# Seven-product down chunks in eight (and five) turns in a row, with two of their weight differences on GpSimd

## The chip, the cores and the metric

The kernel runs on one core of a Trainium2 chip. The metric is the device time of one execution in microseconds (us). Three executions of the kernel before took 1177.59, 1177.66 and 1177.66 us, median 1177.66.

## The reference, cut to what matters

The model is a two-layer decoder trunk on 256 tokens of 1024 features. Each layer has a half SwiGLU block, a mixer, cross-attention and a second half SwiGLU block, so there are four SwiGLU blocks (called f = 0 to 3 here). The change touches only these:

```python
def swiglu(h, w_gate, w_up, w_down):
    return (jax.nn.silu(h @ w_gate) * (h @ w_up)) @ w_down
x = x + 0.5 * swiglu(rmsnorm(x, w), w_gate, w_up, w_down)   # h: (256, 1024), D_FF = 2816
```

All values are float32. The kernel keeps that precision by splitting every operand of a matmul in a rounded high part and a low rest (hi = round(a), lo = a - hi) and by adding three products, hi*hi, hi*lo and lo*hi.

## The kernel before, in words

A SwiGLU block is cut along D_FF into 11 pieces of 256 (FJ = 11). Each piece j has three weight chunks of 1 MB (128 partitions x 2048 float32): gate g(j), up u(j) and down d(j). Chunks come from memory in the order g(j+1), u(j+1), d(j) into a ring of three slots (`raw`), issued by SyncE's queue (L690). ScalarE writes the high part of a chunk (L889), VectorE the low part (L1616, L1586, L1648, L1667), and only then does the slot take the next load: SyncE waits for `lo_done`.

A turn handles one piece. TensorE's turn j + 1 runs g(j+1) (32 matmuls: 16 with 512 columns, L2334, and 16 with 256, L2341), u(j+1) (32 more) and then the down product of d(j) (L2313 to L2315). ScalarE and VectorE run turn j beside it: gate sum (L1514) and scale (L1519), silu, split of g(j+1), up sum (L1525), product (L1533), split of u(j+1), split of the product into `gu_hi` and `gu_lo`, split of d(j). Gate sum and up sum read PSUM and one SBUF tile; the other VectorE operations here read two SBUF tiles.

The down product multiplies the 256x256 piece of the hidden values (2x2 blocks of 128) by the 256x1024 chunk (2x2 blocks of 128x512). Done plainly it takes eight block products, each of three matmuls (24). In a mixed turn (`turn_mixed`, `turn_mixed_next`, `mixed_down`) it takes seven (21 matmuls), by the scheme of Strassen and Winograd. That needs differences of the weight blocks (four `w_sum`s, L1549, 128x512) and of the hidden blocks (four `gu_sum`s, L1555, 128x128), the high and low parts of three weight sums (L900 on ScalarE, L1607 or L1641 on VectorE, 128x1536) and of three hidden sums (L913, L1538, L1636). All eight differences are VectorE's. One of them overwrites a block of the raw chunk in place.

Four of the seven products go to PSUM banks 0 to 3, which the next g and u need. ScalarE copies them out (banks 0 and 1 at L908, 2 and 3 at L918), VectorE does so after the last mixed turn (`mixed_out`, L1566). In blocks 1 to 3 the copies are summed into `xn` by accumulating DMAs of GpSimd's queue (L2269). GpSimd does nothing else in a SwiGLU block; it computes the norms' factors (L2198, L2200) between them.

Which turns are mixed is fixed by `Mixed.FIRST` and `Mixed.COUNT`: in blocks 1 to 3 turns 1, 2, 3, 5, 6, 7 and 8 (turn 4 is plain), in block 0 turns 4, 6 and 8. That makes 24 mixed down products out of 44.

Of the kernel before, what the change touches and what calls it, by code (L numbers as in the profile page):

```python
# [33 lines left out]
FJ = DFF // CW  # L34
# [130 lines left out]
def build(nc, d, out):  # L165
# [3 lines left out]
    with ctx:  # L169
# [274 lines left out]
        class Mixed:  # L444
            FIRST, COUNT = (2, 0, 0, 0), (3, 7, 7, 7)
            w_sums = part(3072, [3, 512])
            gu_sums = part(4608, [3, P])
# [4 lines left out]
            kept = [copied, kept_later, kept_later, kept_later]  # L452
# [53 lines left out]
        w_summed = [quarters_lo] + [es["dtT_done"]] * 3  # L506
        w_sums_hi = [quarters_hi] + [es["ln_done"]] * 3
        gu_summed = [up_half_in] + [es["o_ssq"]] * 3
        mixed_mm = [halves_hi] + [es["dec_mm"]] * 3
        mixed_read = [quarter_in[0]] + [es["kz_done"]] * 3  # L510
        kept_added_in = [sem(f"kept_added_in{half}") for half in range(2)]

        def kept_added_at(f, i):

            return ((f - 1) * (Mixed.COUNT[f] - 2) + i - 1) * 16

        def mixed_end(f):

            return Mixed.FIRST[f] + Mixed.COUNT[f]

        def counted(f, i, each, first, extra=0):

            return (i - Mixed.FIRST[f]) * each + (1 + (f - 1) * (Mixed.COUNT[f] * each + extra) if f else first)

        def w_sums_at(f, i):
            return counted(f, i, 4, 4)

        def w_sums_hi_at(f, i):
            return counted(f, i, 1, 3)

        def gu_sums_at(f, i):
            return counted(f, i, 4, 16)

        def mixed_mm_at(f, i):
            return counted(f, i, 1, 3)

        def mixed_read_at(f, i):
            return counted(f, i, 2, 16, 8)
# [115 lines left out]
        def _(sp):  # L654
# [13 lines left out]
            def ffn(layer, which, first=False):  # L668
                base = at["ffn", layer, which]
# [15 lines left out]
                def turn(j):  # L685
                    for c, (w, width, row) in enumerate(((gate, CW, j + 1), (up, CW, j + 1), (down, D, j))):
                        n = base + 2 + c
                        if not (first and isinstance(j, int) and j == 0 and c == 0):
                            sp.wait_ge(lo_done, j * 3 + (n - RING + 1))
# [8 lines left out]
                if first:  # L698
# [7 lines left out]
                    for j in range(2, 6):  # L706
                        turn(j)
                        for dst, src in tables[3 * (j - 2):3 * (j - 1)]:
                            sp.dma_start(dst, src).then_inc(small_in, 16)
                    for j, (a, b) in ((6, (0, 4)), (7, (4, 7))):  # L710
                        turn(j)
# [3 lines left out]
                with sp.Fori(8 if first else 0, FJ - 1) as j:  # L715
                    turn(j)
# [21 lines left out]
        def _(act):  # L738
# [115 lines left out]
            def ffn(layer, which):  # L854
# [29 lines left out]
                def turn(j, between=lambda c: None, mixed=None, out=None, added=False):  # L884
# [13 lines left out]
                    def sums_hi():  # L898
                        act.wait_ge(w_summed[f], w_sums_at(f, mixed) + 4)
                        nc.scalar.activation(Mixed.w_hi, Mixed.w_sums, ACT.Copy).then_inc(w_sums_hi[f], 1)  # L900

                    if mixed is not None and out is None and f == 0:
                        sums_hi()
                    if out is not None:
                        act.wait_ge(mixed_mm[f], mixed_mm_at(f, out) + 1)
                        if added and (f > 1 or not isinstance(out, int) or out > 1):
                            act.wait_ge(kept_added_in[0], kept_added_at(f, out))
                        nc.scalar.activation((Mixed.copied if added else Mixed.kept[f])[0], ps[:, 0:2, :],  # L908
                                             ACT.Copy).then_inc(mixed_read[f], 1)
                    act.wait_ge(chunks_used, j * 3 + (base + 2))  # L910
                    if mixed is not None:
                        act.wait_ge(gu_summed[f], gu_sums_at(f, mixed) + 4)
                        nc.scalar.activation(Mixed.gu_hi, Mixed.gu_sums, ACT.Copy)  # L913
                    hidden(j + (f * FJ + 1), gu_hi)
                    if out is not None:
                        if added and (f > 1 or not isinstance(out, int) or out > 1):
                            act.wait_ge(kept_added_in[1], kept_added_at(f, out))
                        nc.scalar.activation((Mixed.copied if added else Mixed.kept[f])[1], ps[:, 2:4, :],  # L918
                                             ACT.Copy).then_inc(mixed_read[f], 1)
                    if mixed is not None and (f or out is not None):  # L920
                        sums_hi()
                    split(base + 4 + RING)
# [27 lines left out]
                if f == 0:  # L950
# [5 lines left out]
                         mixed=2)  # L956
                    turn(5, out=2)
                    turn(6, mixed=3)
                    turn(7)
                    turn(8, mixed=4)  # L960
                    turn(9, small_tables)
                else:
                    turn(1, mixed=0)
                    turn(2, mixed=1, out=0)
                    turn(3, mixed=2, out=1, added=True)
                    turn(4, out=2, added=True)
                    turn(5, mixed=3)
                    with act.Fori(4, 7) as i:
                        turn(i + 2, mixed=i, out=i - 1, added=True)
                    turn(9)  # L970
# [382 lines left out]
        def _(dve):  # L1353
# [154 lines left out]
            def ffn(layer, which):  # L1508
# [33 lines left out]
                slot = raw[:, (base + 4) % RING, :].rearrange("p (a c) -> p a c", c=512)  # L1542
                gu_blocks = gu.rearrange("p (a c) -> p a c", c=P)

                def w_sum(i, c, dst, a, b):

                    if c:
                        dve.wait_ge(w_summed[f], w_sums_at(f, i) + c)
                    V.tensor_tensor(dst, a, b, ALU.subtract).then_inc(w_summed[f], 1)  # L1549
# [1616 lines left out]
```

## Time and profile before

| | |
|---|---|
| median of three runs | 1177.66 us |
| span of the profiled execution (first to last instruction) | 1175.6 us |
| TensorE busy | 1169.0 us (99%) |
| VectorE busy | 957.0 us (81%) |
| ScalarE busy | 727.7 us (62%) |
| GpSimd busy | 131.0 us (11%) |

The profile gives for the execution its span and no time of its own beside it; the median is 2.1 us above the span, which lies before the first and after the last instruction. A busy share is an average over the whole kernel. To know what a SwiGLU turn is bound by one reads the turn itself: how long TensorE's turn is, how full VectorE is in it, and how long before its use each part is ready. The page's timeline of the span in 40 slices shows TensorE's granted clock at 9 (90% or more) in every slice.

### The profile page before, as it was taken

The page shows a single profiled execution, that of the slowest core. Times are in us where ns is not written, and L with a number is a line of the kernel's source. Part 1 is how long each engine was busy: PE and PEld are TensorE (multiplying, and loading weights), DVE is VectorE, ACT ScalarE, POOL GpSimd, SP SyncE. Part 2 cuts the span into 40 slices and gives each one's busy share as a digit, 9 for nine tenths or more (in the row PEclk, how much of TensorE's full clock was granted, in tenths as well). Part 3 has the DMA queues.
Part 4 walks back from the last instruction along what each step waited for, and adds up shares of the span by engine and source line. Part 5 has one row for each costly group of instructions (what it writes and reads, how often), then busy time and mean ns, then how long its engine had stood idle before and what let it go on. Part 6 is the DMA issues. An engine that isn't in the chain of part 4 may idle for free.

```text
span 1175.6 us, 17562 instructions
## 1 busy us (share of the span) xinstructions
PE 1169.0 (99%) x6769; PEld 1022.7 (87%) x6769; DVE 957.0 (81%) x1144; ACT 727.7 (62%) x967; POOL 131.0 (11%) x127
## 2 busy tenths in 40 slices
PE   9999999999999999999999999999999999999998
PEld 8888889889989888888888888889887898888886
DVE  6687898875657589889988979997886676797998
ACT  7566555854457566667565757564576566675773
POOL 1010001420142010100010001010012121100000
PEclk9999999999999999999999999999999999999999
DMA  9966755454445455979765779947623434678891
GB/s 322 332 207 199 200 194 179 145 179 144 144 143 180 144 181 173 270 218 268 226 202 166 229 217 263 269 145 213 209 89 135 135 118 156 208 225 251 245 258 69
DMA packets 168337, 230.71 MB, mean 196 GB/s; under 512 B 15312, under 2 KB 139600, under 8 KB 168144
## 3 DMA queue, kind: packets, MB, share of 16 engines
q1 hardware_dynamic: 163664, 213.30, 55.9%
q0 software_dynamic: 4464, 16.25, 7.3%
q8 instruction: 44, 0.72, 0.3%
q10 hardware_dynamic: 144, 0.26, 0.1%
q14 instruction: 21, 0.17, 0.0%
HBM read 213.02 MB, written 1.05 MB: 182 GB/s over the span
## 4 chain that ended last, share of the span: by engine, by line
PE 99%; POOL 0%; DVE 0%; issue 0%; POOLq 0%; DVEq 0%
PE ps L2334 30%; PE ps L2341 16%; PE ps L2313 15%; PE ps L2314 15%; PE ps L2315 15%; PE ps L2417 1%; PE ps L2611 1%; PE ps L3075 1%; PE ps L2931 1%; PE ps L3098 0%; PE ps L2619 0%; PE ps L3111 0%; PE ps L3036 0%; PE ps L3033 0%; PE ps L2485 0%; PE ps L2683 0%
## 5 line engine op out<-in xcount | busy, mean ns | idle before, releaser
L2334 PE MATMUL ps<-hT,w_parts 128*128 128x512 f32 x1568 | 374.9, 391 | 0.0
L2334 PEld LDWEIGHTS ps<-hT,w_parts 128*128 128x128 f32 x1568 | 290.0, 188 | 58.2 <-ACT w_parts L807 0.4
L1368 DVE TENSOR_TENSOR w_parts<-raw,w_parts 128x2048 fp32r<-128x2048 f32 x85 | 196.1, 2316 | 57.9 <-ACT w_parts L754 57.9
L2341 PEld LDWEIGHTS ps<-hT,w_parts 128*128 128x128 f32 x1568 | 201.4, 191 | 8.0 <-DVE w_parts L1444 0.2
L754 ACT ACTIVATE w_parts<-raw 128x2048 fp32r<-128x2048 f32 x85 | 162.3, 1920 | 72.8 <-PE ps L2315 69.8
L889 ACT ACTIVATE w_parts<-raw 128x2048 fp32r<-128x2048 f32 x108 | 206.0, 1907 | 0.6 <-DMA raw<-in_ffn_w_gate 0.6
L2341 PE MATMUL ps<-hT,w_parts 128*128 128x256 f32 x1568 | 204.1, 283 | 0.0
L1616 DVE TENSOR_TENSOR w_parts<-raw,w_parts 128x2048 fp32r<-128x2048 f32 x63 | 143.9, 2284 | 1.2 <-ACT w_parts L889 1.2
L2313 PE MATMUL ps<-w_parts,arena_r 128*128 128x512 f32 (+1 forms) x234 | 91.2, 390 | 0.0
L2314 PE MATMUL ps<-w_parts,arena_r 128*128 128x512 f32 (+1 forms) x234 | 91.1, 389 | 0.0
L2313 PE MATMUL ps<-w_parts,hT 128*128 128x512 f32 (+1 forms) x240 | 91.0, 379 | 0.0
L2315 PE MATMUL ps<-w_parts,arena_r 128*128 128x512 f32 (+1 forms) x234 | 90.6, 387 | 0.0
L2315 PE MATMUL ps<-w_parts,hT 128*128 128x512 f32 (+1 forms) x240 | 90.1, 375 | 0.0
L2314 PE MATMUL ps<-w_parts,hT 128*128 128x512 f32 (+1 forms) x240 | 90.0, 375 | 0.0
L2269 POOL DMA_DIRECT2D xn<-arena x30 | 26.2, 872 | 386.5 <-ACT arena L908 348.9
L869 ACT ACTIVATE arena<-arena 128x512 f32<-128x512 f32 x44 | 27.7, 630 | 55.9 <-DVE arena L1519 55.8
L1667 DVE TENSOR_TENSOR w_parts<-raw,w_parts 128x2048 fp32r<-128x2048 f32 x21 | 48.1, 2289 | 13.9 <-ACT w_parts L889 13.9
L876 ACT ACTIVATE arena<-ps 128x512 f32<-128x512 f32 x44 | 26.3, 597 | 50.1 <-PE ps L2341 49.1
L2198 POOL TENSOR_SCALAR msq<-msum 128x1 f32<-128x1 f32 x18 | 13.4, 742 | 370.9 <-ACT xn L765 288.1
L862 ACT ACTIVATE arena<-ps 128x512 f32<-128x512 f32 x44 | 26.2, 596 | 43.2 <-PE ps L2341 43.0
L2313 PEld LDWEIGHTS ps<-w_parts,hT 128*128 128x128 f32 x240 | 45.2, 188 | 8.4 <-DVE hT L1477 0.4
L2315 PEld LDWEIGHTS ps<-w_parts,hT 128*128 128x128 f32 x240 | 45.2, 188 | 8.3
(375 smaller groups left out, 2123.5 us busy)
## 6 DMA issues: line engine op xcount, KB each, us to landing
raw<-in_ffn_w_down SPq DMA_DIRECT2D x44, 1024.0 KB, 5.0
raw<-in_ffn_w_gate SPq DMA_DIRECT2D x43, 1024.0 KB, 5.4
raw<-in_ffn_w_up SPq DMA_DIRECT2D x43, 1024.0 KB, 5.4
raw<-in_xattn_wkv SPq DMA_DIRECT2D x16, 1024.0 KB, 5.3
xn<-arena POOLq DMA_DIRECT2D x30, 512.0 KB, 5.6
raw<-in_even_w_in SPq DMA_DIRECT2D x13, 1024.0 KB, 5.1
raw<-in_xattn_wq SPq DMA_DIRECT2D x8, 1024.0 KB, 5.1
raw<-in_xattn_wo SPq DMA_DIRECT2D x8, 1024.0 KB, 5.3
```

Source lines behind the costliest of these rows:

```text
L754: ins = nc.scalar.activation(hi, src, ACT.Copy)
L869: nc.scalar.activation(g_act, gate.rearrange("p m c -> p (m c)"), ACT.Silu).then_inc(silu_done, 1)
L876: nc.scalar.activation(up_lo, ps[:, 2:4, SEQ:], ACT.Copy).then_inc(up_copied, 1)
L889: nc.scalar.activation(w_hi[:, m % RING, :], raw[:, m % RING, :], ACT.Copy).then_inc(hi_done, 1)
L1368: ins = V.tensor_tensor(lo, src, hi.bitcast(F32), ALU.subtract)
L1616: V.tensor_tensor(w_lo[:, m % RING, :], raw[:, m % RING, :], w_hi[:, m % RING, :].bitcast(F32), ALU.subtract).then_inc(lo_done, 1)
L1667: V.tensor_tensor(w_lo[:, m % RING, :], raw[:, m % RING, :], w_hi[:, m % RING, :].bitcast(F32), ALU.subtract).then_inc(lo_done, 1)
L2313: mm(dst, l_hi, r_hi, start=start, stop=False)
L2314: mm(dst, l_hi, r_lo, start=False, stop=False)
L2315: return mm(dst, l_lo, r_hi, start=False, stop=stop)
L2334: mm(ps[:, bank0 + m, :], cols(w_hi, n, k, CW, m * P, (m + 1) * P), hT[:, k, :, :].rearrange("p a c -> p (a c)"), start=k == 0, stop=False)
L2341: last = mm(ps[:, bank0 + m, SEQ:], cols(w_lo, n, k, CW, m * P, (m + 1) * P), hT[:, k, 0, :], start=False, stop=k == KT - 1)
```

## The change: what it does

- Mixed turns are now turns 4 to 8 in block 0 (five in a row) and 1 to 8 in blocks 1 to 3 (eight in a row). That makes 29 mixed down products.
- GpSimd computes two of the four weight differences, `w_first` = block 0 - block 1 (into a free part of `xk`) and `w_sums[0]` = block 2 - block 0. VectorE computes the other two. The raw chunk is no longer overwritten.
- `w_first` takes the place of block 0 in the chunk's high and low parts, so the split of a mixed d(j) is in two: blocks 1 to 3 straight from the raw chunk (1536 columns), block 0 from `w_first` (512 columns), on ScalarE and on VectorE.
- SyncE's next d load waits for `down_split`, the low part of blocks 1 to 3, instead of the whole split.
- VectorE has one order of a mixed turn for all blocks: the four hidden differences right after the product, then the split of u(j+1), then two weight differences, the hidden low parts, and the three low parts of the chunk.
- ScalarE makes the high part of blocks 1 to 3 ahead of that of the weight sums and of `w_first`.
- Block 0 now sums its copies in `xn` by accumulating DMAs too; there are 12 more of them (42 instead of 30). GpSimd's `norm(1)` (the memory's norm factors) now stands behind `ffn(0)` in its queue.
- The blocks of the seven products and their banks are permuted; `kept_added` adds the halves in another order.

```diff
-            FIRST, COUNT = (2, 0, 0, 0), (3, 7, 7, 7)
+            TURN, COUNT = (4, 1, 1, 1), (5, 8, 8, 8)
+            w_first = xk[:, 6:8, :].rearrange("p a c -> p (a c)")
-            kept = [copied, kept_later, kept_later, kept_later]
+            kept = kept_later
...
+                        if c == 2 and after_mixed:
+                            behind = Mixed.TURN[f] + 1
+                            sp.wait_ge(down_split, j + (down_split_at(f, 0) + 1 - behind))
...
+                    if mixed is None:
+                        split(base + 4 + RING)
+                    else:
+                        m = (base + 4) % RING
+                        act.wait_ge(raw_in[m], (j - 1) * 16 + landed(base + 4 + RING))
+                        nc.scalar.activation(w_hi[:, m, 512:], raw[:, m, 512:], ACT.Copy).then_inc(hi_done, 1)
+                        act.wait_ge(w_summed, mixed * 4 + (w_sums_at(f, 0) + 4))
+                        nc.scalar.activation(Mixed.w_hi, Mixed.w_sums, ACT.Copy)
+                        nc.scalar.activation(w_hi[:, m, 0:512], Mixed.w_first, ACT.Copy).then_inc(w_sums_hi, 1)
...
                     gu_sum(i, 2, Mixed.gu_sums[:, 1, :], gu_blocks[:, 1, :], gu_blocks[:, 0, :], ALU.subtract)
-                    dve.wait_ge(raw_in[m % RING], (j - 1) * 16 + landed(m))
+                    gu_sum(i, 3, Mixed.gu_sums[:, 2, :], gu_blocks[:, 2, :], Mixed.gu_sums[:, 1, :], ALU.subtract)
+                    split(base + 3 + RING)
+                    n, m = base + 4 + RING, (base + 4) % RING
+                    dve.wait_ge(w_summed, i * 4 + (w_sums_at(f, 0) + 2))
                     dve.wait_ge(lo_done, j * 3 + (base + 2))
-                    w_sum(i, 0, Mixed.w_sums[:, 0, :], slot[:, 3, :], slot[:, 1, :])
-                    gu_sum(i, 3, Mixed.gu_sums[:, 2, :], gu_blocks[:, 2, :], Mixed.gu_sums[:, 1, :], ALU.subtract)
-                    w_sum(i, 1, slot[:, 1, :], slot[:, 1, :], slot[:, 0, :])
-                    w_sum(i, 2, Mixed.w_sums[:, 1, :], slot[:, 3, :], slot[:, 1, :])
-                    w_sum(i, 3, Mixed.w_sums[:, 2, :], slot[:, 2, :], Mixed.w_sums[:, 1, :])
+                    V.tensor_tensor(Mixed.w_sums[:, 1, :], raw[:, m, 1024:1536], Mixed.w_first,
+                                    ALU.subtract).then_inc(w_summed, 1)
+                    dve.wait_ge(w_summed, i * 4 + (w_sums_at(f, 0) + 3))
+                    V.tensor_tensor(Mixed.w_sums[:, 2, :], raw[:, m, 1536:], Mixed.w_sums[:, 1, :],
+                                    ALU.subtract).then_inc(w_summed, 1)
+                    hidden_lo(j, gu_hi, gu_lo, mixed=True)
+                    dve.wait_ge(hi_done, (j - 1) * 3 + (n + 1))
+                    dve.wait_ge(w_summed, i * 4 + (w_sums_at(f, 0) + 4))
+                    V.tensor_tensor(w_lo[:, m, 512:], raw[:, m, 512:], w_hi[:, m, 512:].bitcast(F32),
+                                    ALU.subtract).then_inc(down_split, 1)
+                    dve.wait_ge(w_sums_hi, i + (w_sums_hi_at(f, 0) + 1))
                     V.tensor_tensor(Mixed.w_lo, Mixed.w_sums, Mixed.w_hi.bitcast(F32), ALU.subtract)
+                    V.tensor_tensor(w_lo[:, m, 0:512], Mixed.w_first, w_hi[:, m, 0:512].bitcast(F32),
+                                    ALU.subtract).then_inc(lo_done, 1)
...
+                for i in range(Mixed.COUNT[f]):
+                    n = n0 + 3 * (Mixed.TURN[f] + i)
+                    pool.wait_ge(raw_in[n % RING], landed(n))
+                    pool.wait_ge(lo_done, n - RING + 1)
+                    w_sum(i, 0, Mixed.w_first, blocks[:, 0, :], blocks[:, 1, :])
+                    w_sum(i, 1, Mixed.w_sums[:, 0, :], blocks[:, 2, :], blocks[:, 0, :])
+                    if i > 1:
+                        for half in range(2):
+                            pool.wait_ge(mixed_read, mixed_read_at(f, i - 1) + half + 1)
...
             norm(0)
+            ffn(0)
             norm(1)
...
-                turn(5, False, kept=3)
-                turn(6, False, mixed=3)
+                turn(first, False, mixed=0)
+                with pe.Fori(1, Mixed.COUNT[f]) as i:
+                    turn(i + first, False, kept=i, mixed=i)
```

## Rows read from the trace of the kernel before

**Rows 1.** The page, part 1: busy us (share of the span) and instructions of each engine
```profile
PE 1169.0 (99%) x6769; PEld 1022.7 (87%) x6769; DVE 957.0 (81%) x1144; ACT 727.7 (62%) x967; POOL 131.0 (11%) x127
```
**Rows 2.** Waits of TensorE: us in total, times, longest
```profile
PE ps L3111 <- POOL neg_half L2272: 0.9, 1, 0.9
```
**Rows 3.** Busy time in one plain turn, then one mixed turn, of TensorE
```profile
core 0: us, PE busy (x) PEld busy (x) DVE busy (x) ACT busy (x) POOL busy (x), PEclk, DMA share, GB/s
434.12:450.69 16.57, 16.57 (x90) 14.35 (x89) 13.82 (x19) 9.71 (x9) 0.00 (x0) 1.00 0.39 128
732.11:748.00 15.89, 15.89 (x86) 13.78 (x86) 15.53 (x19) 11.57 (x12) 1.72 (x2) 1.00 0.96 265
```
**Rows 4.** The chain that ended last, 700 to 770: start us, us, what
```profile
748.00 3.65 PE ps L2334 x16
...
753.57 0.23 PE ps L2313
```
**Rows 5.** Groups of instructions: line, engine, shapes | busy us, mean ns | idle before
```profile
L889 ACT ACTIVATE w_parts<-raw 128x2048 fp32r<-128x2048 f32 x108 | 206.0, 1907 | 0.6 <-DMA raw<-in_ffn_w_gate 0.6
L1616 DVE TENSOR_TENSOR w_parts<-raw,w_parts 128x2048 fp32r<-128x2048 f32 x63 | 143.9, 2284 | 1.2 <-ACT w_parts L889 1.2
L1641 DVE TENSOR_TENSOR mixed_parts<-arena,mixed_parts 128x1536 fp32r<-128x1536 f32 x21 | 36.8, 1750 | 0.0
L900 ACT ACTIVATE mixed_parts<-arena 128x1536 fp32r<-128x1536 f32 x24 | 35.8, 1490 | 15.5 <-DVE arena L1549 15.5
L1549 DVE TENSOR_TENSOR arena<-raw 128x512 f32<-128x512 f32 x48 | 33.2, 691 | 3.1 <-DMA raw<-in_ffn_w_down 2.4
L869 ACT ACTIVATE arena<-arena 128x512 f32<-128x512 f32 x44 | 27.7, 630 | 55.9 <-DVE arena L1519 55.8
```
**Rows 6.** Timeline, one mixed turn: start us, us, engine, line, what
```profile
735.52 0.68 DVE L1514 TENSOR_TENSOR arena<-arena,ps 128x512 f32<-128x512 f32 x1
...
739.05 0.68 DVE L1525 TENSOR_TENSOR arena<-arena,ps 128x512 f32<-128x512 f32 x1
739.92 0.69 DVE L1533 TENSOR_TENSOR arena<-arena 128x512 f32<-128x512 f32 x1 [0.19 <-DVE arena L1525]
...
743.53 1.00 ACT L918 ACTIVATE arena<-ps 128x1024 f32<-128x1024 f32 x1
...
749.21 2.29 DVE L1616 TENSOR_TENSOR w_parts<-raw,w_parts 128x2048 fp32r<-128x2048 f32 x1
751.41 0.68 DVE L1514 TENSOR_TENSOR arena<-arena,ps 128x512 f32<-128x512 f32 x1
```
**Rows 7.** Timeline where GpSimd and VectorE work together, 325 to 376
```profile
328.69 5.85 POOL L2212 TENSOR_TENSOR xk_parts<-xk,arena_r 128x512 fp32r<-128x512 f32 x3
...
330.08 3.31 DVE L1368 TENSOR_TENSOR w_parts<-raw,w_parts 128x2048 fp32r<-128x2048 f32 x1 [2.51 <-ACT w_parts L754]
...
367.31 7.62 POOL L2219 TENSOR_TENSOR xv_parts<-xv,xn_parts 128x512 fp32r<-128x512 f32 x4 [14.44 <-ACT xn_parts L1018]
...
367.78 1.37 DVE L1777 TENSOR_TENSOR q_parts<-arena,q_parts 128x512 fp32r<-128x512 f32 x1 [2.52 <-ACT q_parts L1014]
369.07 0.68 DVE L1756 TENSOR_REDUCE arena<-ps 128x2 f32<-128x512 f32 x1
```
**Rows 8.** Groups: a GpSimd operation of 512 columns
```profile
L2230 POOL TENSOR_TENSOR xn<-x,xk 128x512 f32<-128x512 f32 x1 | 1.3, 1280 | 0.8 <-DVE x L1494 0.8
```
**Rows 9.** DMA issues: KB each, median us from issue to landing
```profile
raw<-in_ffn_w_down SPq DMA_DIRECT2D x44, 1024.0 KB, 5.0
xn<-arena POOLq DMA_DIRECT2D x30, 512.0 KB, 5.6
```
**Rows 10.** GpSimd's timeline around the memory's norm
```profile
83.04 2.43 POOL L2198 TENSOR_SCALAR msq<-msum 128x1 f32<-128x1 f32 x1 [61.40 <-ACT xv L765]
...
187.49 0.30 POOL L2198 TENSOR_SCALAR msq<-msum 128x1 f32<-128x1 f32 x1 [94.16 <-ACT xn L765]
```

More of the change, by code:

```diff
@@ L706, in ffn @@
                     for j in range(2, 6):
-                        turn(j)
+                        turn(j, j > Mixed.TURN[f])
                         for dst, src in tables[3 * (j - 2):3 * (j - 1)]:
@@ L714, in ffn @@
                                 sp.dma_start(dst, src).then_inc(small_in, 16)
-                with sp.Fori(8 if first else 0, FJ - 1) as j:
-                    turn(j)
+                    turn(8, True)
+                    turn(9, True)
+                else:
+                    turn(0)
+                    turn(1)
+                    with sp.Fori(2, FJ - 1) as j:
+                        turn(j, True)
                 n = base + FFN_CHUNKS - 1
@@ L897, in turn, with copied @@
                     between(1)
[L898 to L903, printed above, removed]
-                    if out is not None:
[L905 to L909, printed above, removed]
+                    def copied(half):
+                        if added:
+                            if f or not isinstance(out, int) or out > 1:
+                                act.wait_ge(kept_added_in[half], out * 16 + kept_added_at(f, 0))
+                        nc.scalar.activation((Mixed.copied if added else Mixed.kept)[half], ps[:, 2 * half:2 * half + 2, :],
+                                             ACT.Copy).then_inc(mixed_read, 1)
+                    if out is not None:
+                        act.wait_ge(mixed_mm, out + (mixed_mm_at(f, 0) + 1))
+                        copied(0)
                     act.wait_ge(chunks_used, j * 3 + (base + 2))
                     if mixed is not None:
-                        act.wait_ge(gu_summed[f], gu_sums_at(f, mixed) + 4)
+                        act.wait_ge(gu_summed, mixed * 4 + (gu_sums_at(f, 0) + 4))
                         nc.scalar.activation(Mixed.gu_hi, Mixed.gu_sums, ACT.Copy)
@@ L915, in turn @@
                     if out is not None:
[L916 to L922, printed above, removed]
+                        copied(1)
+                    if mixed is None:
+                        split(base + 4 + RING)
+                    else:
+                        m = (base + 4) % RING
[4 more added lines that the diff above has]
+                        nc.scalar.activation(w_hi[:, m, 0:512], Mixed.w_first, ACT.Copy).then_inc(w_sums_hi, 1)
                     between(2)
@@ L955, in ffn @@
                     turn(4, lambda c: c and squares(1, mem_rows, lambda t, h: act.wait_ge(mem_in, 16), tiles=(c - 1,)),
[L956 to L961, printed above, removed]
+                         mixed=0)
                 else:
                     turn(1, mixed=0)
[L964 to L970, printed above, removed]
+                first = Mixed.TURN[f]
+                turn(first + 1, mixed=1, out=0)
+                turn(first + 2, mixed=2, out=1, added=True)
+                with act.Fori(3, Mixed.COUNT[f]) as i:
+                    turn(i + first, mixed=i, out=i - 1, added=True)
+                if f == 0:
+                    turn(FJ - 2, small_tables)
+                else:
+                    turn(FJ - 2)
                 made[0] = base + FFN_CHUNKS - 1
@@ L2404, in mixed_down @@
                     if bank == 1:
-                        last.then_inc(mixed_mm[f], 1)
+                        last.then_inc(mixed_mm, 1)
                 return last
@@ L2551, in turn @@
                     if kept is not None:
[L2552 removed]
+                        pe.wait_ge(mixed_read, kept * 2 + mixed_read_at(f, 0))
                     pe.wait_ge(up_read, j + f * FJ)
@@ L2577, in ffn @@
                 turn(1, True)
+                first = Mixed.TURN[f] + 1
                 if f == 0:
[L2579 removed]
+                    with pe.Fori(2, first) as j:
                         turn(j, False)
[L2581 to L2594 removed]
+                turn(first, False, mixed=0)
+                with pe.Fori(1, Mixed.COUNT[f]) as i:
+                    turn(i + first, False, kept=i, mixed=i)
+                turn(FJ - 1, False, held=f == 3, kept=Mixed.COUNT[f])
                 n = base + FFN_CHUNKS - 1
```

167 lines of the change are left out of this document (51 added, 116 removed).

## The prediction

> **What bounds the kernel now.** I read four views, from the whole to one turn. The page's busy row [rows 1] has TensorE busy for 1169.0 us of a span of 1175.6 us, and the view of waits [rows 2] has a single wait of TensorE in the whole kernel, 0.9 us at the start. So TensorE never waits in a SwiGLU block: time is gained only by giving it fewer matmuls, and lost only if some other engine becomes late. The windows [rows 3] put a number on a turn: 16.57 us with a plain down product (434.12 to 450.69, before the first mixed one of its block) and 15.89 us with seven products, TensorE busy throughout in both. The difference of 0.68 us is three matmuls of 0.23 us, as the chain of waits prices each [rows 4].
>
> The same windows show who is next. In the mixed turn VectorE is busy 15.53 of 15.89 us and the rest is its waits on its own results (0.19 us ahead of L1533 [rows 6]); from gate sum to gate sum it needs 751.41 - 735.52 = 15.89 us [rows 6], as much as TensorE. ScalarE is at 11.57 us. So mixed turns in a row have no room on VectorE today; the question of this change is whether VectorE stays under 15.89 us a turn, and how far it may fall behind before TensorE notices.
>
> **The change part by part.**
>
> *TensorE.* Mixed products go from 3 + 7 + 7 + 7 = 24 to 5 + 8 + 8 + 8 = 29. Five turns less 0.68 us [rows 3] are -3.4 us, all on the path, since TensorE is the path. The permuted blocks and banks have the same matmuls: 0.
>
> *VectorE's own work in a mixed turn.* Two weight differences go: 2 x 0.69 = -1.38 us (L1549) [rows 5]. The split of 2048 columns (2.28, L1616) becomes one of 1536 (1.75, as L1641 of the same size) and one of 512 (0.69): +0.16 us. So 15.89 - 1.38 + 0.16 = 14.7 us, 1.2 us below TensorE's turn. The other operations are moved, not added.
>
> *ScalarE.* Its split becomes 1.49 (L900's size) + 0.63 (L869's) instead of 1.91 [rows 5]: +0.2 us on 11.57 us [rows 3]. Hidden by its idle 4 us.
>
> *How early the down chunk is ready.* Before, the split of d(j) ends at 749.21 + 2.29 = 751.5, and TensorE starts on it at 753.57 [rows 4, 6]: 2.1 us ahead. After: ScalarE ends the second copy of the kept banks at 744.5 (743.53 + 1.00 [rows 6]). Then come the high parts of blocks 1 to 3 (1.5), of the weight sums (1.5) and of `w_first` (0.6), to about 748.1; VectorE's last two low parts end at about 748.1 + 0.7 at the earliest, and by VectorE's own order (1.75 + 1.75 + 0.69 from the first high part on) at 746.0 + 4.2 = 750.2. So the chunk is ready by 750.2, 3.3 us ahead of its use. These 3.3 us are a reserve for a whole block: only when VectorE has fallen behind by more than that does TensorE stand still.
>
> *GpSimd's two differences.* This is the unknown cost. Alone an operation of this size takes 1.28 us [rows 8]. But the timeline shows the two engines excluding each other [rows 7]. A VectorE split of 2.29 us takes 3.31 us when a GpSimd operation had begun ahead of it (+1.02); a 512-column operation with two SBUF inputs takes 1.37 instead of 0.69 [rows 5] (+0.68); and four GpSimd operations take 7.62 us instead of 4 x 1.28 = 5.12. The reduction at 369.07, which reads PSUM, keeps its 0.68 us. So a GpSimd difference costs VectorE something only if it meets an operation with two SBUF inputs, and then at most its own length.
> The cost a turn lies between 0 (both in VectorE's idle time) and 2 x 1.28 = 2.56 us. Where they fall follows from the load. d(j+1) is issued after the low part of blocks 1 to 3 and lands 5.0 us later [rows 9]. In that time VectorE does two low parts (1.75 + 0.69), gate sum, scale and is in the split of g (0.68 + 0.69 + 2.28), 6.1 us in all. So GpSimd finds the chunk landed while VectorE splits g and begins when that split ends, beside the up sum, which reads PSUM and takes 739.92 - 739.05 = 0.87 us with the wait behind it [rows 6]. The first difference is nearly covered (0.2 us left); the second meets the product or the hidden differences and costs about 1.0 us, the nearest row being the +1.02. I take 1.2 us: VectorE's turn is 14.7 + 1.2 = 15.9 us, level with TensorE, and the reserve of 3.3 us stays whole. Cost: 0.
> The Trainium skill, "SBUF — State Buffer", section "Who interferes with whom", says that a VectorE instruction with two SBUF inputs contends with a GpSimd instruction that reads SBUF, the first keeping the shared ports for its whole length, and one with at most one SBUF input does not. The trace agrees (+1.02, +0.68 and 0). "Perfetto Trace Analysis", section "Optimizing Scalar/DVE Operations", draws from it that moving work between these two might not help; by that rule the saved 1.38 us come back as up to 2.56 us, which is the slower rival below.
>
> *The wait for GpSimd.* VectorE now waits for both differences before its own two, and behind it stand the hidden low parts and the down chunk's. In rows 6 the up sum begins at 739.05; with it (0.87), the product (0.73), four hidden differences (about 1.1) and the split of u (2.28) VectorE comes there at 744.0. GpSimd begins at the latest beside that up sum. Even if each difference has to sit out a split it is done by 739.05 + 2 x (2.29 + 1.28) = 746.2, 2.2 us late, inside the reserve. Cost 0, at most the excess over 3.3 us.
>
> *Queues.* SyncE's d load goes out earlier than its old wait let it (the two last low parts are not waited for), so the order of three loads a turn is kept and none is later. GpSimd's 12 more accumulating DMAs land in 5.6 us [rows 9] against 15.89 us to the next; they follow the differences in its queue but wait for ScalarE's copies that come later anyway. Load on the DMA engines: they are at 0.96 in a mixed turn today [rows 3] without a wait of TensorE; a block has that now for all its turns. `norm(1)` moves from 83 us to behind block 0's last accumulating DMA, about 165 us; its four small operations, at 2.43 us each as the one on the timeline [rows 10], are done by 175 us, and GpSimd's next work is at 187.5 [rows 10]. 0.
>
> *Sum.* Against the profiled span: 1175.6 - 3.4 = 1172.2 us. The median of the runs is 2.1 us above the span, so 1177.66 - 3.4 = 1174.3 us.
>
> **The rivals.**
>
> *A: small stalls.* GpSimd's differences cost VectorE more like 1.65 us, as when neither is covered by the up sum but both are of the +0.68 to +1.02 kind. VectorE's turn is then 16.35 us, 0.46 late a turn, 3.7 us after eight turns; 0.4 us above the reserve in each of three blocks, 1.2 us lost. The same class holds a late landing in block 0, where small tables share SyncE's queue, or an accumulating DMA that a copy waits for, 1 to 2 us once or twice. For it: several waits now hang on GpSimd. Against it: the 3.3 us. Time: 1175.5 to 1177.5, I take 1176.3.
>
> *B, slower: VectorE becomes the bound.* Both differences meet two-input operations at full price, 2 x 1.02: VectorE's turn is 14.7 + 2.04 = 16.74 us, 0.85 late a turn. Eight turns are 6.8 us, 3.5 above the reserve, in three blocks 10.5 us; five turns in block 0 4.3 us, 1.0 above. Together 11.5 - 3.4 = +8.1: 1185.8 us; at 2.56 us a turn 1201. It makes the kernel slower from the point where 3 x (8e - 3.3) = 3.4, e = 0.55 us, that is a VectorE turn over 16.44 us or GpSimd's differences over 1.75 us of VectorE's time. For it: VectorE is packed, so once it is late nearly every operation after the up sum has two SBUF inputs. Against it: when it is late the up sum waits for nobody, so one difference always finds it, and a late VectorE still issues the load at the same distance from it.
>
> *C: the change doesn't do what it says.* Fewer turns than 29 last 15.89 us, because the first or last turn of a block has to wait for its differences. Time about 1177.5.
>
> **How the numbers follow.** The forecast has 0.71, A 0.15, B 0.11, C 0.03. A measurement of this kernel can tell 0.2% (2.4 us) from no change, so faster means under 1175.3. The forecast's own range is 1173.7 to 1175.3. Faster: 0.71 and a little of A, 0.72; same: the rest of A and C, 0.16; slower: B and a tail of A, 0.12. The range goes from 1173.7 (0.6 us for what a turn's length may differ by) over all of A to 1178.0; B is left out.
>
> **What would show it.** Right: TensorE turns of 15.89 us in all 29 places, no new wait of TensorE; VectorE with a turn of 15.9 us or less, and with low parts of d(j) ending 1 us or more ahead of L2313's first matmul. GpSimd's differences last 1.3 us beside the up sum and up to 3.5 us where they start in a split. Wrong: TensorE waiting for `w_parts` or `mixed_parts` of VectorE in the later turns of a block (A or B, told apart by the turn from which it begins), or VectorE operations of 0.69 us that last 1.4 or more twice a turn.

## The result, and the profile after

The changed kernel takes 1189.28 us (median; 1188.7 to 1189.7), the kernel before 1177.66. The ratio is 1.0098, with a 95% interval of 1.0084 to 1.0112: it is slower by 1.0%. The forecast was 1174.3 us. The profiled execution has a span of 1186.8 us, 11.2 us more than before.

The page's busy row after, and then the three largest new waits of TensorE (columns as in [rows 1, 2]):

```profile
PE 1172.4 (99%) x6754; PEld 1018.4 (86%) x6754; DVE 991.5 (84%) x1163; ACT 748.2 (63%) x1018; POOL 224.9 (19%) x197
```
```profile
PE ps L2308 <- ACT arena L907: 3.0, 4, 1.3
PE ps L2287 <- DVE arena L1517: 2.0, 5, 0.4
PE ps L2308 <- DVE xn L1561: 1.7, 3, 0.6
```

TensorE has 15 instructions fewer, five turns less three matmuls. But these three waits are new: for ScalarE's copies of the kept banks (L907), for the gate sum (L1517) and for VectorE's own copy of the kept banks at the end of a block (L1561). They add up to 6.7 us and are only part of what was lost. The rest is gaps too short for that view, and is found by the length of the turns. In block 1, TensorE's timeline shows where each g begins (start us, us, engine, line, what, idle before):

```profile
509.58 3.79 PE L2308 MATMUL ps<-hT,w_parts 128*128 128x512 f32 x16
...
525.72 3.90 PE L2308 MATMUL ps<-hT,w_parts 128*128 128x512 f32 x16
...
542.67 3.93 PE L2308 MATMUL ps<-hT,w_parts 128*128 128x512 f32 x16
...
560.25 3.92 PE L2308 MATMUL ps<-hT,w_parts 128*128 128x512 f32 x16 [0.61 <-ACT arena L907]
...
577.01 3.88 PE L2308 MATMUL ps<-hT,w_parts 128*128 128x512 f32 x16 [0.58 <-DVE xn L1561]
```

The first four mixed turns of the block last 15.89 us as forecast. The last four last 16.14, 16.95, 17.58 and 16.76 us. Added up over each block, against the same block before less its saved turns, the standing time is 2.0 us in block 0 and 3.9, 4.1 and 3.8 us in blocks 1 to 3: 13.8 us. With the 3.4 us saved that is +10.4, of the 11.2 us by which the span grew; the other 0.8 us lie outside the blocks' turns.

VectorE's timeline says why: the second mixed turn of block 1, and then the fourth (same columns):

```profile
457.95 0.69 DVE L1528 TENSOR_TENSOR arena<-arena,ps 128x512 f32<-128x512 f32 x1 [0.76 <-ACT arena L881]
458.83 1.32 DVE L1536 TENSOR_TENSOR arena<-arena 128x512 f32<-128x512 f32 x1 [0.19 <-DVE arena L1528]
460.18 1.27 DVE L1551 TENSOR_TENSOR arena<-arena 128x128 f32<-128x128 f32 x4
461.37 2.28 DVE L1581 TENSOR_TENSOR w_parts<-raw,w_parts 128x2048 fp32r<-128x2048 f32 x1
...
486.25 0.68 DVE L1517 TENSOR_TENSOR arena<-arena,ps 128x512 f32<-128x512 f32 x1
...
491.37 3.22 DVE L1551 TENSOR_TENSOR arena<-arena 128x128 f32<-128x128 f32 x4
494.50 2.28 DVE L1581 TENSOR_TENSOR w_parts<-raw,w_parts 128x2048 fp32r<-128x2048 f32 x1
...
503.04 0.68 DVE L1517 TENSOR_TENSOR arena<-arena,ps 128x512 f32<-128x512 f32 x1
```

The turn is 503.04 - 486.25 = 16.79 us, 0.90 more than TensorE's. The four hidden differences (L1551) take 494.50 - 491.37 = 3.13 us in it and 461.37 - 460.18 = 1.19 us where nothing is beside them: 1.94 us of the turn are lost there, and VectorE's own work is 16.79 - 1.94 = 14.85 us. Beside them stand GpSimd's two differences, in GpSimd's and SyncE's timelines (same columns; L690 issues a chunk's load, L2242 an accumulating transfer):

```profile
480.26 0.86 POOL L2242 DMA_DIRECT2D xn<-arena  x1 [2.49 <-ACT arena L907]
491.40 1.41 POOL L2229 TENSOR_TENSOR xk<-raw 128x512 f32<-128x512 f32 x1 [10.28 <-DMA raw<-in_ffn_w_down]
492.77 1.33 POOL L2229 TENSOR_TENSOR arena<-raw 128x512 f32<-128x512 f32 x1
```
```profile
480.02 0.37 SPq L690 DMA_DIRECT2D raw<-in_ffn_w_up  x1
484.24 0.37 SPq L690 DMA_DIRECT2D raw<-in_ffn_w_down  x1
```

The down chunk goes out at 484.24 and GpSimd can start at 491.40, 7.2 us later and not 5.0. The load is this late from the fourth mixed turn of a block on. The first three down loads of a block's mixed turns have no accumulating transfer ahead of them. Issues in the windows 450:470 and 501:552 (KB each, median us to landing):

```profile
raw<-in_ffn_w_down SPq DMA_DIRECT2D x2, 1024.0 KB, 4.7
raw<-in_ffn_w_down SPq DMA_DIRECT2D x4, 1024.0 KB, 7.6
```

In blocks 1 to 3 these first three land in 4.7 to 4.9 us and the later ones in 6.9 to 7.8. The window of such a late turn (columns as in [rows 3]) has room on ScalarE:

```profile
487.06:503.04 15.98, 15.98 (x88) 13.87 (x87) 15.62 (x16) 11.58 (x12) 4.36 (x4) 1.00 0.87 247
```

The page's list of DMA issues has the whole kernel (KB each, median us to landing). Its 6.6 us for the down chunk lies between the two groups, and no single load took it:

```profile
raw<-in_ffn_w_down SPq DMA_DIRECT2D x44, 1024.0 KB, 6.6
raw<-in_ffn_w_gate SPq DMA_DIRECT2D x43, 1024.0 KB, 5.2
raw<-in_ffn_w_up SPq DMA_DIRECT2D x43, 1024.0 KB, 6.4
xn<-arena POOLq DMA_DIRECT2D x42, 512.0 KB, 6.7
```

The down chunk took 5.0 us before and the accumulating transfers 5.6 [rows 9]. The groups of instructions place what it costs (busy us, mean ns):

```profile
L1581 DVE TENSOR_TENSOR w_parts<-raw,w_parts 128x2048 fp32r<-128x2048 f32 x58 | 138.0, 2379 | 0.4 <-ACT w_parts L894 0.4
L1551 DVE TENSOR_TENSOR arena<-arena 128x128 f32<-128x128 f32 x116 | 63.3, 546 | 4.0
...
L1536 DVE TENSOR_TENSOR arena<-arena 128x512 f32<-128x512 f32 x44 | 36.6, 833 | 8.7 <-DVE arena L1528 4.8 <-ACT arena L874 2.6
```

A split is 2284 ns where GpSimd is idle [rows 5], a product 692 (its median in both of the first two experiments) and a hidden difference 292.

### The profile page after: what moved, and what is told of

It is laid out like the page before. It is cut to its first block and busy times, and to the rows that moved or that the text cites. A ratio compares the mean times of both kernels' runs of the same rounds, so it can differ in the third digit from the quotient of the medians.

```text
span 1186.8 us, 17925 instructions
## 1 busy us (share of the span) xinstructions
PE 1172.4 (99%) x6754; PEld 1018.4 (86%) x6754; DVE 991.5 (84%) x1163; ACT 748.2 (63%) x1018; POOL 224.9 (19%) x197
## 5 line engine op out<-in xcount | busy, mean ns | idle before, releaser
L1371 DVE TENSOR_TENSOR w_parts<-raw,w_parts 128x2048 fp32r<-128x2048 f32 x85 | 195.9, 2315 | 57.9 <-ACT w_parts L759 57.9
L759 ACT ACTIVATE w_parts<-raw 128x2048 fp32r<-128x2048 f32 x85 | 162.1, 1920 | 72.8 <-PE ps L2289 70.3
L894 ACT ACTIVATE w_parts<-raw 128x2048 fp32r<-128x2048 f32 x79 | 150.9, 1910 | 4.7 <-DMA raw<-in_ffn_w_up 4.3
L1581 DVE TENSOR_TENSOR w_parts<-raw,w_parts 128x2048 fp32r<-128x2048 f32 x58 | 138.0, 2379 | 0.4 <-ACT w_parts L894 0.4
L2229 POOL TENSOR_TENSOR xk<-raw 128x512 f32<-128x512 f32 x29 | 46.4, 1599 | 400.9 <-DMA raw<-in_ffn_w_down 400.9
L2287 PE MATMUL ps<-w_parts,arena_r 128*128 128x512 f32 (+1 forms) x209 | 82.1, 393 | 2.0 <-DVE arena L1517 2.0
L2288 PE MATMUL ps<-w_parts,arena_r 128*128 128x512 f32 (+1 forms) x209 | 81.4, 389 | 0.0
L2289 PE MATMUL ps<-w_parts,arena_r 128*128 128x512 f32 (+1 forms) x209 | 81.0, 387 | 0.0
L1551 DVE TENSOR_TENSOR arena<-arena 128x128 f32<-128x128 f32 x116 | 63.3, 546 | 4.0
L881 ACT ACTIVATE arena<-ps 128x512 f32<-128x512 f32 x44 | 26.0, 592 | 46.8 <-PE ps L2315 46.8
L916 ACT ACTIVATE mixed_parts<-arena 128x384 fp32r<-128x384 f32 x29 | 15.3, 526 | 61.7 <-DVE arena L1551 38.9
```

The costliest lines, as they stand in the source:

```text
L759: ins = nc.scalar.activation(hi, src, ACT.Copy)
L894: nc.scalar.activation(w_hi[:, m % RING, :], raw[:, m % RING, :], ACT.Copy).then_inc(hi_done, 1)
L1371: ins = V.tensor_tensor(lo, src, hi.bitcast(F32), ALU.subtract)
L1551: V.tensor_tensor(dst, a, b, op).then_inc(gu_summed, 1)
L1581: V.tensor_tensor(w_lo[:, m % RING, :], raw[:, m % RING, :], w_hi[:, m % RING, :].bitcast(F32), ALU.subtract).then_inc(lo_done, 1)
L2229: G.tensor_tensor(dst, a, b, ALU.subtract).then_inc(w_summed, 1)
```

## The experiments

The theory was: GpSimd's reads hold up VectorE by 1.9 us a turn, because the chunk lands late, and it lands late because of the accumulating transfers. The rivals: VectorE's own order or its waits for GpSimd make it late; the rows of eight mixed turns do; SyncE's queue does. Each ratio is against executions of the kernel before taken beside that experiment (medians of 1177.43 to 1177.53 us).

**All four differences on VectorE.** The changed kernel with GpSimd's two taken away:

```diff
-                    dve.wait_ge(w_summed, i * 4 + (w_sums_at(f, 0) + 2))
+                    dve.wait_ge(raw_in[m], (j - 1) * 16 + landed(n))
+                    V.tensor_tensor(Mixed.w_first, raw[:, m, 0:512], raw[:, m, 512:1024], ALU.subtract)...
+                    V.tensor_tensor(Mixed.w_sums[:, 0, :], raw[:, m, 1024:1536], raw[:, m, 0:512], ALU.subtract)...
```

> All four weight differences on VectorE, everything else as in the changed kernel. Theory 'port' (each GpSimd difference stops VectorE for its own length, about 1.05 us, once the two meet an operation with two SBUF inputs): VectorE's turn is its own work, 14.7 + 1.4 = 16.1 us, 0.2 us over TensorE's turn, 1.7 us after eight turns, below the reserve of about 3 us; all 29 turns last 15.89 us and the time is 1177.7 - 3.4 = 1174.3 us. Rival 'row' (eight mixed turns in a row are too many for the copies, the loads and the new order of VectorE, whoever makes the differences): VectorE has more work than in the changed kernel, so the time is 1189 us or more.

Measured: 1179.22 us (1178.37 to 1180.38), ratio 1.0016 (1.0007 to 1.0025). Ten of the 11.6 us are gone, so nearly all of the loss hangs on GpSimd. It is not the forecast time: the hidden differences are back at 292 ns, but VectorE's turn is 16.18 us (14.85 + 2 x 0.69 = 16.23), 0.29 late a turn, and that alone makes TensorE stand still at the end of blocks, for VectorE's copy:

```profile
PE ps L2308 <- DVE xn L1561: 1.7, 3, 0.6
```

In block 1 its seven turns from the second mixed one on take 113.76 us (gate sums at 452.09 and 565.85) where TensorE's take 7 x 15.89 = 111.23. So it is 2.5 us late and TensorE loses 1.15: the reserve is about 1.4 us, not 3.3.

**GpSimd writes only.** Its two subtractions become fills of the same size, with all waits as they were; the weight differences are left out.

```diff
-                    G.tensor_tensor(dst, a, b, ALU.subtract).then_inc(w_summed, 1)
+                    G.memset(dst, 0.25).then_inc(w_summed, 1)
```

> GpSimd's two differences are replaced by two fills of the same tiles with a constant: same place in its queue, same waits before and after, but no reads of SBUF (the weight differences are left out of the computation). Port theory: VectorE is not stopped, its turn is at most TensorE's, hidden differences take 1.1 us again, time 1174.3 us. Rival 'wait' (VectorE is late because it waits for a chunk that lands late and for GpSimd's queue): the waits are all there, so the time stays near 1189 us.

Measured: 1174.86 us (1174.47 to 1176.18), ratio 0.9978 (0.9969 to 0.9987). VectorE's groups (as above):

```profile
L1581 DVE TENSOR_TENSOR w_parts<-raw,w_parts 128x2048 fp32r<-128x2048 f32 x58 | 132.5, 2285 | 1.0 <-ACT w_parts L894 1.0
L1551 DVE TENSOR_TENSOR arena<-arena 128x128 f32<-128x128 f32 x116 | 33.9, 292 | 3.9
```

The chunk still lands after 6.9 us and every wait still stands, and all turns of blocks 1 to 3 are back at 15.89 us (TensorE still loses 1.1 us in block 0). So there the late chunk by itself costs nothing: the loss needs GpSimd's reads. A fill takes 0.53 us and a difference 1.28, so this run shortens GpSimd's work too; but two fills beside the hidden differences don't lengthen those at all. By the Trainium skill, "SBUF — State Buffer", section "Who interferes with whom", a VectorE instruction with two SBUF inputs contends with GpSimd's reads and not with GpSimd's writes alone; this trace agrees, 292 ns against 546.

**One of the two on GpSimd.** The second moves to VectorE (the wait and one `tensor_tensor` as in the first experiment).

> One difference on GpSimd, three on VectorE. Port theory: VectorE's turn is 14.7 + 0.7 + 1.05 = 16.45 us, 0.55 a turn over TensorE; eight turns are 4.4 us, 1.1 to 1.4 above the reserve of 3.0 to 3.3, in three blocks 3.3 to 4.2 us: 1177.6 to 1178.5 us. If only the second of two back-to-back differences costs anything (the first being covered): 15.5 us a turn and 1174.3 us. Row theory: 1189 us.

Measured: 1182.23 us (1181.94 to 1182.81), ratio 1.0041 (1.0026 to 1.0057). VectorE's turn is 16.43 to 16.59 us, as expected, but the time is 4 us above what was expected from it, since that took a reserve of 3.0 to 3.3 us. Counted as in the first experiment, VectorE is 4.1 us late in block 1 and TensorE loses 2.0, which makes 2.1.

**Tiny accumulating transfers.** Both halves are cut to 8 of 512 columns (the rest of the kept products' sum is left out).

```diff
-                            pool.dma_start(Mixed.kept[half], Mixed.copied[half],
+                            pool.dma_start(Mixed.kept[half][:, :, 0:8], Mixed.copied[half][:, :, 0:8],
```

> The accumulating DMAs of GpSimd's queue move 8 of 512 columns a block (the rest of the sum is left out), the differences stay on GpSimd. Theory 'late landing': the down chunk lands in 5.0 instead of 6.6 us after its issue, GpSimd starts beside the up sum, VectorE loses 1.2 us a turn instead of 2.1, its turn is 15.9 us, time 1174 to 1176 us. If the place does not matter (VectorE is packed, so the port costs 2 x 1.05 wherever the differences fall): 1187 to 1189 us.

Measured: 1175.05 us (1174.87 to 1175.29), ratio 0.9979 (0.997 to 0.9989), with both differences still on GpSimd. The chunk lands in 4.8 us, and each turn costs VectorE 0.23 us in the product and 0.98 in the hidden differences: 1.21 us, and a turn of 16.05. Every mixed turn of TensorE is 15.89 us, though VectorE is 1.7 us late at the end of block 1 (counted as before). This is nearly the forecast's turn, and nearly its time.

**Only the second transfer tiny.** A turn has two, each for one half of the kept banks; the same cut for half 1 alone.

> The changed kernel with one edit: only the second of a turn's two accumulating transfers is cut to 8 of its 512 columns (the rest of its sum is left out). It is issued within 4 us of the u and down loads. If it is this one that delays the down chunk, the chunk lands in about 5 us, VectorE's turn is near 16.05 us as with both cut, and the time is 1175 to 1176.5 us. If it is the first, the chunk still takes 6.5 us and the time stays near 1187 us. If each does half, about 1180 us with landings of 5.7 us.

Measured: 1175.10 us (1174.98 to 1175.32), ratio 0.9979 (0.997 to 0.9988). So it is the second one, which goes out at 480.26, between the loads of u and d. Without it, GpSimd's and VectorE's timelines are (same columns):

```profile
487.12 2.04 POOL L2229 TENSOR_TENSOR xk<-raw 128x512 f32<-128x512 f32 x1 [7.54 <-DMA raw<-in_ffn_w_down]
489.12 1.74 POOL L2229 TENSOR_TENSOR arena<-raw 128x512 f32<-128x512 f32 x1
```
```profile
487.92 0.68 DVE L1528 TENSOR_TENSOR arena<-arena,ps 128x512 f32<-128x512 f32 x1
488.78 0.92 DVE L1536 TENSOR_TENSOR arena<-arena 128x512 f32<-128x512 f32 x1 [0.19 <-DVE arena L1528]
489.73 2.25 DVE L1551 TENSOR_TENSOR arena<-arena 128x128 f32<-128x128 f32 x4
```

GpSimd's first difference waits out the split of g and then runs beside the up sum, which reads PSUM and keeps its 0.68 us. Of the first VectorE pays 0.23 us, in the product, and of the second 0.98, in the hidden differences: the 0.2 and about 1.0 us of the forecast. One 512 KB transfer a turn decides over 14 us.

**The second transfer later.** It is issued only when the next down chunk has landed.

```diff
+                    if i > 2:
+                        added(i - 1, 1)
...
-                        for half in range(2):
+                        added(i, 0)
```

> The changed kernel with the second accumulating DMA of a turn issued only when the next down chunk has landed, ahead of GpSimd's two differences. Theory 'late landing': the chunk lands in 5 us again, the differences begin as the split of g ends, VectorE loses about 1.2 us a turn instead of 2.1, time 1174.5 to 1176.5 us. If the accumulating DMAs are not what delays the chunk: 1187 to 1190 us.

Measured: 1192.5 us (1189.53 to 1193.7), ratio 1.0121 (1.0106 to 1.0137). The chunk does land in 5.0 us, but the time is far from the 1174.5 to 1176.5 us expected, for two reasons (VectorE's timeline):

```profile
506.08 3.14 DVE L1536 TENSOR_TENSOR arena<-arena 128x512 f32<-128x512 f32 x1 [0.19 <-DVE arena L1528]
...
515.64 1.76 DVE L1606 TENSOR_TENSOR w_parts<-raw,w_parts 128x1536 fp32r<-128x1536 f32 x1 [0.52 <-ACT w_parts L925]
```

Both GpSimd differences now come ahead of the waiting product, which takes 3.14 us instead of 0.69, since GpSimd issues the transfer first and begins at 505.80, 0.5 us behind the end of the split of g; and ScalarE's second copy of the kept banks must wait for the later transfer, so the high parts are late (0.52) and TensorE waits 2.8 us for L907. The load that now follows the transfer, g's, lands in about 8.2 us instead of 5.2, without a wait for it. The mend gives back elsewhere what it wins.

**The down load later.** The changed kernel with the load's old wait, for the whole split, so that it goes out some 2.3 us later.

```diff
-                        if c == 2 and after_mixed:
+                        if c == 2 and after_mixed and False:
```

> The changed kernel with one edit: the load of the down chunk again waits for the old, later event, and so goes out about 2.3 us later. Theory (late landing puts GpSimd's two subtractions beside VectorE's hidden differences): the chunk then lands 2 us later still unless the transfers before it have ended, and GpSimd runs beside the split or the copies of the low halves; the port costs 1 to 2.1 us a turn and the time is 1187 to 1192 us. Rival (it is the early issue itself that brings the load together with the accumulating transfer): the load lands in about 5 us again, at the same moment as now (1189 us). Neither gives a time under 1185.

Measured: 1200.16 us (1198.64 to 1200.63), ratio 1.0189 (1.0173 to 1.0204), 8 us above the upper end. The median landing is 4.9 us, but in the turn with the gate sum at 523.85 the load goes out at 524.11 and GpSimd starts at 529.10, 5.25 us behind the gate sum; in the changed kernel it was 491.40 - 486.25 = 5.15 us. So the earlier issue of the change buys nothing in a usual turn. Where VectorE is late as well it does, as GpSimd's and VectorE's timelines show:

```profile
547.00 3.39 POOL L2229 TENSOR_TENSOR xk<-raw 128x512 f32<-128x512 f32 x1 [11.66 <-DMA raw<-in_ffn_w_down]
```
```profile
551.79 0.69 DVE L1598 TENSOR_TENSOR arena<-raw,xk 128x512 f32<-128x512 f32 x1 [2.56 <-POOL arena L2229]
```

GpSimd has to wait out the split of u, and VectorE then waits 2.56 us for GpSimd: the turn is 17.5 us. The forecast put that wait at zero for the changed kernel, where it is 2.5 us in all; it is the next cost in line.

**Only turn 4 mixed.** The kernel before, with blocks 1 to 3 mixed in turns 1 to 8 and block 0 as it was: 27 mixed turns, VectorE's old order, nothing on GpSimd.

```diff
-            FIRST, COUNT = (2, 0, 0, 0), (3, 7, 7, 7)
+            FIRST, COUNT = (2, 0, 0, 0), (3, 8, 8, 8)
```

> The kernel before with turn 4 of blocks 1 to 3 made a mixed turn too (27 seven-product chunks, eight in a row), all differences on VectorE in its old order, nothing on GpSimd. TensorE's term alone: 3 x 0.68 = 2.0 us less, 1175.6 us, if VectorE's old turn of 15.9 us (level with TensorE's) does not drift in eight turns. Rival 'row' (eight in a row are too many as such): VectorE, which is packed, falls behind by 0.1 us or more a turn and TensorE waits at the end of each block: 1177 us or more.

Measured: 1175.89 us (1175.53 to 1176.13), ratio 0.9985 (0.9976 to 0.9994). Three turns gave 1.6 us and the forecast's 0.68 each would be 2.0. TensorE's only wait is the old one of 0.9 us. Eight mixed turns in a row are no problem in themselves.

**All 29 in the old order.** The same, with turns 4 to 8 of block 0 as well, and its copies summed by accumulating transfers.

```diff
-            FIRST, COUNT = (2, 0, 0, 0), (3, 7, 7, 7)
+            FIRST, COUNT = (0, 0, 0, 0), (5, 8, 8, 8)
-            kept = [copied, kept_later, kept_later, kept_later]
+            kept = [kept_later] * 4
```

> The kernel before with the changed kernel's 29 mixed turns (five and eight in a row, block 0 summing in xn by accumulating DMAs), but VectorE's old order and all four differences on it, the chunk split whole. If the count of mixed turns was never the trouble: 1177.5 - 3.4 = 1174.1 us, faster than both. Rival: block 0's turns, which had slack from plain turns between, stall: 1175 to 1177 us.

Measured: 1177.25 us (1177.01 to 1181.09), ratio 1.0003 (0.9994 to 1.0012). Blocks 1 to 3 have 15.89 us throughout. Block 0 stands still for 2.9 us in two turns in a row (18.09 and 16.62 us). SyncE's and ScalarE's timelines:

```profile
126.75 4.74 SPq L714 DMA_DIRECT2D pe_pairs<-in_nsa_cmp_pe  x2
131.86 0.78 SPq L690 DMA_DIRECT2D raw<-in_ffn_w_gate  x1
```
```profile
144.28 1.92 ACT L889 ACTIVATE w_parts<-raw 128x2048 fp32r<-128x2048 f32 x1 [5.20 <-DMA raw<-in_ffn_w_gate]
```

Two loads of small tables, element by element, hold SyncE for 4.7 us, and the gate chunk behind them is split from 144.28 on, 12.4 us after its issue.

**The tables earlier.** The kernel of the last experiment, with those loads in turn 3 of block 0, ahead of its mixed turns.

```diff
-                            for dst, src in tables[3 * (j - 2):3 * (j - 1)]:
+                            for dst, src in (strided_loads()[4:7] if j == 3 else tables[3 * (j - 2):3 * (j - 1)]):
...
-                            for dst, src in strided_loads()[a:b]:
+                            for dst, src in (strided_loads()[0:4] if j == 6 else tables[3:6]):
```

> The kernel with the old order of VectorE's turn and rows of 5, 8, 8 and 8 mixed turns (1177.25 us), with one edit: the element-wise pair and convolution loads on SyncE's queue go out in turn 3 of block 0 and no longer in turn 7, ahead of which the gate load of 131.86 stood waiting. If these loads cost block 0 its 3.4 us, the stall at 138 goes and the time is 1177.5 - 3.4 = 1174.1 us (1173.7 to 1174.7), with every mixed turn of block 0 at 15.9 us. If block 0's loss comes from its accumulating transfers or from something else, it stays at 1177 us and the gap stays at the same turn.

Measured: 1175.27 us (1174.96 to 1175.65), ratio 0.998 (0.9971 to 0.9989), 2.0 us less than the experiment before; the span of the profiled execution is 1172.9 against 1175.6, and all but 0.2 us of block 0's loss is gone from it. The time is 0.6 us above the range of 1173.7 to 1174.7 expected; 0.4 us went to a new wait of TensorE in a norm. It beats both kernels, and is the fastest here that leaves nothing out; from the one with only turn 4 (1175.89) it can't be told, as the two intervals overlap. In the changed kernel with a tiny second transfer block 0 loses nothing either, with the tables in their old place: the loss needed both.

**GpSimd's reads beside the old order.** The 29-turn kernel in the old order, with two GpSimd subtractions of constants in each mixed turn of blocks 1 to 3 that nobody reads.

```diff
+                        for c in range(2):
+                            step(G.tensor_tensor(unread, consts[:, 0:512], consts[:, 512:1024], ALU.subtract))
```

> The suspected cost alone: the kernel of e7_old_order_5_8_8_8 plus, in the 24 mixed turns of blocks 1 to 3, two GpSimd subtractions of 512 columns that read constants and whose results nobody reads or waits for, begun when the down chunk lands. Port theory: each stops VectorE for about 1.05 us, and VectorE had no spare time: 24 x 2.1 = 50 us less a reserve of about 1 us a block, so 1174 + 47 = 1221 us; if one of the two is covered by the up sum, 24 us and 1197 us. If the loss of the changed kernel came from waiting for GpSimd's results and not from the port: 1174 us, as without them.

Measured: 1232.78 us (1232.4 to 1233.13), ratio 1.0467 (1.0451 to 1.0483): 55.5 us over 24 turns, 2.3 us a turn, for work that nothing waits for, and 12 us above the 1221 expected. GpSimd began the two not as the chunk landed but behind a block's second accumulating transfer, beside the split of d (VectorE's timeline):

```profile
501.36 3.72 DVE L1611 TENSOR_TENSOR w_parts<-raw,w_parts 128x2048 fp32r<-128x2048 f32 x1
505.01 2.85 DVE L1636 TENSOR_TENSOR mixed_parts<-arena,mixed_parts 128x1536 fp32r<-128x1536 f32 x1
```

The split has 1.44 us on top and the low part 1.10, 2.54 us a turn. With no slack on VectorE nearly all of it comes out in the time.

## Why the prediction was wrong, step by step

*TensorE's saving* was right: 15.89 us where TensorE doesn't stand still, and 3.4 us over five turns.

*VectorE's own work* was right within 0.15 us: 14.85, forecast 14.7. *ScalarE's* 0.2 us too: 11.58 us in a turn, with room left.

*GpSimd's two differences* is the step that failed. The mechanism stood in the text and held, but from the fourth mixed turn of a block on the size was 1.94 us a turn and up to 2.1, where 1.2 was taken, above the 1.75 from which the text had the kernel slower. The 1.2 rested on the chunk landing 5.0 us after its issue, the median of the kernel before. In its mixed turns that have one, the second accumulating transfer goes out 6.8 us ahead of the down load. In the plain turn of block 1 it goes out 4.0 us ahead, and there the trace already had the late landing (GpSimd's and SyncE's timelines, and the issues in the window 498:503, as above):

```profile
494.71 0.86 POOL L2269 DMA_DIRECT2D xn<-arena  x1 [2.15 <-ACT arena L918]
```
```profile
498.72 0.37 SPq L690 DMA_DIRECT2D raw<-in_ffn_w_down  x1
```
```profile
raw<-in_ffn_w_down SPq DMA_DIRECT2D x1, 1024.0 KB, 8.5
```

Blocks 2 and 3 have the same, 7.9 and 8.3 us, and the median hides all three. The change makes this distance the usual one (480.26 and 484.24), and the chunk came 1.9 to 2.8 us later. GpSimd then began at the hidden differences, past the up sum that was to cover the first one. With that transfer cut the landing is 4.8 us and the cost 1.21 us, the forecast's own figure. The sentence that a late VectorE issues the load at the same distance from itself is true and did not help: in every late turn the two meet at the same wrong place.

*How early the down chunk is ready* was right for the down chunk and wrong as a reserve. TensorE never waits for the chunk after the change. It waits for banks, for L907, for L1517 and, at the end of a block, for VectorE's own copy L1561, which leaves less room. By the experiments the room is 1.4 us (no difference on GpSimd) and 2.1 (one); in block 1 of the changed kernel VectorE falls 5.7 us behind (seven turns of 16.33 to 16.95 us against 15.89) and loses 3.9, which makes 1.8. With 3.3 us the same turns would have cost 2.4 us a block.

*The wait for GpSimd* was forecast as late but hidden. It occurs once, as 2.5 us of idle VectorE in block 0; whether that reaches TensorE isn't shown, as no run takes this wait away alone. *Queues* was wrong: "the order of three loads a turn is kept and none is later" looked at the order and not at what shares the DMA engines. *norm(1)*: no new wait on it.

*Rival B* described what happened. It had 16.74 us a turn (measured 16.79 in block 1's middle) and 1185.8 us, 3.5 too low. In blocks 1 to 3 it has VectorE 6.8 us late with 3.3 in reserve, which costs 3.5 a block; block 1 has 5.7 and 1.8, which costs 3.9. That it comes so near is in part luck, since the two errors nearly cancel. What it lacks is 1.3 us in these three blocks, 1.0 in block 0, 0.8 outside the blocks' turns and 0.4 by which the median lies further above the span than before. It was given 0.11 because the up sum "always finds" one difference, which holds only for a chunk that has landed by then. *Rival A*'s late landing beside the small tables of block 0 did come, in the 29-turn kernel in the old order.

Not shown is why the second transfer slows the load. The two share the DMA engines, and a share of 0.87 busy in such a turn leaves open whether it is their bandwidth or the transfer's read and write of the same place.

## What to carry to other kernels

Work moved from VectorE to GpSimd was free here only beside VectorE operations that read PSUM or in VectorE's idle time, so the moment at which GpSimd's input lands is a term of the sum; take that landing time with the transfers that will be in the air then, not the median of the kernel before, and look at the single landings that this median hides. Compute the reserve from every buffer that the busiest engine waits for, the banks at the end of a loop among them, and not from the one that the change touches.

## What the runs showed of the hardware beside that

- Two GpSimd operations in a row can both go ahead of a VectorE operation that waits: a product of 0.69 us took 3.14 us (the second transfer later), which is more than one GpSimd operation of 1.3 us.
- The exclusion also lengthens GpSimd: a difference of 1.28 us takes 2.04 where it meets the end of a split, and 3.39 where it meets its start.
- Short VectorE operations are held up too: four of 0.29 us lost 1.94 us to two of GpSimd, 0.97 to each, where a split of 2.28 us lost 1.44 us to one and the low part behind it 1.10 to the next.
- A late 1 MB load: ready 12.4 us after its issue, behind two small element-wise loads and with an accumulating transfer in the air; the median landing of such a load is 5.2 us.
- How close the 512 KB accumulating transfer goes out decides the landing: issued 6.8 us ahead of a down load it left it at 4.9 to 5.4 us (kernel before, blocks 1 to 3), issued 3.9 to 5.3 us ahead it moved it to 6.9 to 7.8 (changed kernel, blocks 1 to 3). Issued just ahead of a gate load it moved that one from 5.2 to about 8.2 us (the second transfer later).
